# Attention by pairs of heads: two heads' scores in the row halves of the array, their values in its column halves

## What is computed

```python
for window, dilation in DILATED_PATTERNS:          # ((128, 1), (512, 4), (2048, 16))
    o, lse = dilated_window_attention(q, k, v, window, dilation)
...
wts = jax.nn.softmax(jnp.stack(lses), axis=0)
return jnp.einsum('gbsh,gbshd->bshd', wts, jnp.stack(outs))
```

```python
logits = jnp.einsum('bqhgd,bqkhd->bqhgk', qb, ksel).astype(jnp.float32) * att_scale
logits = jnp.where(valid[:, :, None, None, :], logits, -jnp.inf)
prob = jax.nn.softmax(logits, axis=-1)
return jnp.einsum('bqhgk,bqkhd->bqhgd', prob.astype(vsel.dtype), vsel)
```

## Time and profile before

| | us |
|---|---|
| Median of 3 runs | 2689.79 |
| Lowest and highest | 2689.01, 2691.61 |
| The profiled execution, its own time | 2689.53 |
| Its span, first to last instruction | 2687.7 |
| TensorE busy in it | 2562.5 (95%) |
| VectorE, ACT, GpSimd busy | 1155.4, 879.4, 947.8 |
| Mean granted clock of TensorE | 0.976 |

### The profile page before, as it was taken

One profiled execution on the slowest core, in us unless ns is written; L12 is line 12 of the kernel. 1 busy time (PEld: TensorE's weight loads), 2 busy tenths in 40 slices (PEclk: granted clock), 3 DMA queues, 4 the chain that ended last, 5 costly groups with the idle time before them and its releaser, 6 DMA issues.

```text
span 2687.7 us, 29655 instructions
## 1 busy us (share of the span) xinstructions
PE 2562.5 (95%) x11731; PEld 2033.4 (76%) x11731; DVE 1155.4 (43%) x1638; ACT 879.4 (33%) x1102; POOL 947.8 (35%) x205
## 2 busy tenths in 40 slices
PE   5999899999999999899999999989799889999998
PEld 4757688888888757688888887878575578888887
DVE  4445655430312445655430413447585445433301
ACT  4244333431323244333431323341324323322213
POOL 2312234444444312234444443431232134444442
PEclk8999999999999999999999999989899899999999
DMA  3212122222223212122222323220122122222231
GB/s 129 79 32 63 63 77 96 89 99 94 94 94 98 79 32 63 63 79 94 92 96 94 94 94 94 80 63 24 56 76 63 36 79 94 94 94 94 94 102 70
DMA packets 174012, 215.16 MB, mean 80 GB/s; under 512 B 7644, under 2 KB 155028, under 8 KB 173908
## 3 DMA queue, kind: packets, MB, share of 16 engines
q1 hardware_dynamic: 171412, 209.86, 24.3%
q10 hardware_dynamic: 2496, 3.83, 0.4%
HBM read 211.19 MB, written 2.10 MB: 79 GB/s over the span
## 4 chain that ended last, share of the span: by engine, by line
issue 62%; PE 22%; POOL 13%; DVE 1%; ACT 0%; POOLq 0%; DVEq 0%; ACTq 0%
POOL w_lo L276 13%; PE ps L706 6%; PE ps L306 3%; PE ps L307 3%; PE ps L308 3%; PE ps L1694 1%; PE ps L1690 1%; PE ps L1692 1%; PE ps L847 1%; PE ps L826 1%; PE ps L836 0%; DVE s_window L2279 0%; PE ps L2252 0%; POOLq L278 0%; DVE s_pooled L2292 0%
## 5 line engine op out<-in xcount | busy, mean ns | idle before, releaser
L276 POOL TENSOR_TENSOR w_lo<-w_raw,w_hi 128x2048 fp32r<-128x2048 f32 x201 | 947.6, 4715 | 1712.9 <-ACT w_hi L267 1712.9
L267 ACT ACTIVATE w_hi<-w_raw 128x2048 fp32r<-128x2048 f32 x201 | 384.8, 1915 | 1087.9 <-PE ps L308 393.3
L706 PE MATMUL ps<-h_hi,w_hi 128*128 128x512 f32 (+1 forms) x936 | 403.3, 431 | 9.2 <-POOL w_lo L276 5.8
L706 PE MATMUL ps<-h_hi,w_lo 128*128 128x512 f32 (+1 forms) x936 | 374.9, 401 | 0.0
L706 PE MATMUL ps<-h_lo,w_hi 128*128 128x512 f32 (+1 forms) x936 | 374.9, 400 | 0.0
L306 PE MATMUL ps<-h_hi,w_hi 128*128 128x512 f32 x816 | 319.0, 391 | 0.0
L308 PE MATMUL ps<-h_hi,w_lo 128*128 128x512 f32 x816 | 317.5, 389 | 0.0
L307 PE MATMUL ps<-h_lo,w_hi 128*128 128x512 f32 x816 | 317.4, 389 | 0.0
L706 PEld LDWEIGHTS ps<-h_hi,w_hi 128*128 128x128 f32 (+1 forms) x936 | 179.9, 192 | 66.9 <-issue 24.4
L706 PEld LDWEIGHTS ps<-h_lo,w_hi 128*128 128x128 f32 (+1 forms) x936 | 179.9, 192 | 44.5 <-issue 8.6
L706 PEld LDWEIGHTS ps<-h_hi,w_lo 128*128 128x128 f32 (+1 forms) x936 | 179.3, 192 | 43.0
(11 more groups left out here) (399 smaller groups left out, 3935.9 us busy)
## 6 DMA issues: line engine op xcount, KB each, us to landing
w_raw<-in_w_in SPq DMA_DIRECT2D x72, 1024.0 KB, 5.2
w_raw<-in_w_ff SPq DMA_DIRECT2D x64, 1024.0 KB, 5.2
w_raw<-in_w_ffn_in SPq DMA_DIRECT2D x22, 1024.0 KB, 5.0
w_raw<-in_w_out SPq DMA_DIRECT2D x12, 1024.0 KB, 5.1
w_raw<-in_w_ffn_out SPq DMA_DIRECT2D x11, 1024.0 KB, 4.9
w_raw<-in_w_proj_att SPq DMA_DIRECT2D x4, 1024.0 KB, 5.0
w_raw<-in_w_proj_mlstm SPq DMA_DIRECT2D x4, 1024.0 KB, 5.1
w_raw<-in_w_up_ssd SPq DMA_DIRECT2D x4, 1024.0 KB, 5.3
```

Of the source, the lines that this page charges most:

```text
L267: act.activation(k.whi[:, slot * SLOT:(slot + 1) * SLOT], k.wraw[:, slot * SLOT:(slot + 1) * SLOT], ACT.Copy).then_inc(k.hi_done, 1)
L276: pool.tensor_tensor(k.wlo[:, a:a + SLOT], k.wraw[:, a:a + SLOT], k.whi[:, a:a + SLOT], ALU.subtract).then_inc(k.split, 1)
L706: mm = pe.matmul(out, lhs, rhs, start=i == 0 and n == 0, stop=stop and n == 2)
```

## The change

A step is now a pair of heads and a block of queries: 16 steps and 2 or 3 more to drain. The two score matmuls of a pair (L823) follow each other with one semaphore increment on the second, into banks 4 and 5. The value matmuls of both heads (L834) alternate over the blocks of keys, both into bank 7, one head to partitions 0 to 63 and the other to 64 to 127. The transposes (L847) of both heads of step n - 1 stand in step n, each waiting for its multiply and for the copy before. The scores of step n wait for both masks of step n - 1. VectorE has both masks of step n (L867), one reciprocal for both heads of step n - 1 (L874) and its two multiplies (L880). ACT has both exps of step n (L900), the high part of an ended pair (L907) and both copies of step n - 1 (L917). The low part (L885) and the high part are made once a pair over 128 partitions. The side pieces are shared out over three places in each step: behind the scores, behind the place of the values, and between the transposes of the two heads. The budgets are the same.

```diff
     def pe(self, pe):
...
-        for n in range(self.N + 4):
+        for n in range(self.N + 2):
             if n < self.N:
-                h, i = divmod(n, TT)
-                if n >= 2:
-                    pe.wait_ge(*self.at("masked", n - 1))
-                pe.matmul(k.ps[:, 4 + n % 2, 0:(i + 1) * P], self.q(h)[:, i * P:(i + 1) * P],
-                          self.kk(h)[:, 0:(i + 1) * P], start=True, stop=True)\
-                  .then_inc(self.sem("scores"), 1)
-            m = n - 3
+                p, i = divmod(n, TT)
+                if n:
+                    pe.wait_ge(*self.at("masked", 2 * n))
+                for j in range(2):
+                    mm = pe.matmul(k.ps[:, 4 + j, 0:(i + 1) * P], self.q(2 * p + j)[:, i * P:(i + 1) * P],
+                                   self.kk(2 * p + j)[:, 0:(i + 1) * P], start=True, stop=True)
+                mm.then_inc(self.sem("scores"), 1)
+            self.side_pe(pe, 3 * n, self.steps)
+            p = self.ended(n - 2)
+            if p is not None:
+                pe.wait_ge(*self.at("copied", 2 * (n - 1)))
+                if p:
+                    pe.wait_ge(*self.at("lo", p))
+                for b in range(TT):
+                    for j in range(2):
+                        mm = pe.matmul(k.ps[j * HD:(j + 1) * HD, 7, b * P:T], self.v(b, 2 * p + j),
+                                       self.pt[:, (j * TT + b) * T + b * P:(j * TT + b + 1) * T],
+                                       start=b == 0, stop=b == TT - 1, skip_group_check=True)
+                mm.then_inc(self.sem("values"), 1)
+            self.side_pe(pe, 3 * n + 1, self.steps)
+            m = n - 1
             if 0 <= m < self.N:
...
+                for j in range(2):
+                    pe.wait_ge(*self.at("probs", 2 * m + j + 1))
+                    if 2 * m + j:
+                        pe.wait_ge(*self.at("copied", 2 * m + j))
+                    buf = (2 * m + j) % 4 * T
+                    for b in range(m % TT + 1):
+                        tr = pe.transpose(k.ps[:, 6, b * P:(b + 1) * P],
+                                          self.p[:, buf + b * P:buf + (b + 1) * P], k.const(C_ID))
+                    tr.then_inc(self.sem("turned"), 1)
+                    if j == 0:
+                        self.side_pe(pe, 3 * n + 2, self.steps)
...
     def dve(self, dve):
...
                 dve.wait_ge(*self.at("scores", n + 1))
...
+                for j in range(2):
+                    if n:
+                        dve.wait_ge(*self.at("exp", 2 * (n - 1) + j + 1))
+                    c = 2 * n + j
+                    dve.tensor_tensor_reduce(self.ns[:, j * T:j * T + w], k.ps[:, 4 + j, 0:w],
+                                             self.mask(n % TT), 1.0, BIG, ALU.add, ALU.min,
+                                             self.stat[:, c:c + 1]).then_inc(self.sem("masked"), 1)
```

More of the change, by code:

```diff
@@ L796, in __init__ @@
         super().__init__(k, name, prev)
[L797 removed]
+        self.q, self.kk, self.v, self.mask, self.yhi, self.ylo, self.bias = q, kk, v, mask, yhi, ylo, bias
         self.ns = k.at(f"{name}_negscores", ns, 2 * T)
@@ L800, in __init__, with ended, tile @@
         self.pt = k.at(f"{name}_probsT", scr + 4 * T, 2 * TT * T)
-        self.N, self.bias = HEADS * TT, bias
+        self.pairs = HEADS // 2
+        self.N = self.pairs * TT
         self.stat = k.stat
-        self.ends = [self.at("lo", HEADS)]
+        self.ends = [self.at("lo", self.pairs)]
+        self.steps = 3 * (self.N + 2)
     def tally(self):
[L808 to L816, removed]
+        return {**{name: 2 * self.N for name in ("masked", "exp", "probs", "turned", "copied")},
+                "scores": self.N, "recip": self.N, "values": self.pairs, "hi": self.pairs, "lo": self.pairs}
+    def ended(self, n):
+        return n // TT if n >= 0 and n % TT == TT - 1 else None
+    def tile(self, x, p):
+        return x[:, p * T:(p + 1) * T]
     def pe(self, pe):
@@ L889, in act @@
         self.join(act)
[L890 to L891 removed]
+        for n in range(self.N + 2):
+            self.side_out("act", act, 3 * n, self.steps)
             if n < self.N:
                 w = (n % TT + 1) * P
[L894 to L917 removed]
@@ new lines, in act @@
+                for j in range(2):
+                    c = 2 * n + j
+                    act.wait_ge(*self.at("masked", c + 1))
+                    if n >= 2:
+                        act.wait_ge(*self.at("turned", c - 3))
+                    act.activation(self.p[:, c % 4 * T:c % 4 * T + w], self.ns[:, j * T:j * T + w],
+                                   ACT.Exp, bias=self.stat[:, c:c + 1], scale=-1.0,
+                                   accum_out=self.stat[:, 32 + c:33 + c]).then_inc(self.sem("exp"), 1)
@@ new lines, in act @@
+            p = self.ended(n - 2)
+            if p is not None:
+                act.wait_ge(*self.at("values", p + 1))
+                more = {"bias": self.bias(p)} if self.bias else {}
+                act.activation(self.tile(self.yhi, p), k.ps[:, 7, :], ACT.Identity if self.bias else ACT.Copy,
+                               **more).then_inc(self.sem("hi"), 1)
+            m = n - 1
+            if 0 <= m < self.N:
+                p, i = divmod(m, TT)
+                for j in range(2):
+                    act.wait_ge(*self.at("turned", 2 * m + j + 1))
+                    if p and i == 0:
+                        act.wait_ge(*self.at("values", p))
+                    dst = self.pt[:, j * TT * T:(j + 1) * TT * T].rearrange("p (b q) -> p b q", b=TT)
+                    act.activation(dst[:, 0:i + 1, i * P:(i + 1) * P],
+                                   k.ps[:, 6, 0:(i + 1) * P].rearrange("p (b q) -> p b q", q=P),
+                                   ACT.Copy).then_inc(self.sem("copied"), 1)
```

86 lines of the change are left out of this document (18 added, 68 removed).

## The result

The changed kernel takes 2665.32 us (median of 4 runs, 2658.33 to 2668.49) against 2690.70 of the kernel before (4 runs, 2689.01 to 2691.71): a ratio of 0.9903, 95% interval 0.9882 to 0.9923, faster by 1.0%. In six more runs it stood at 0.9928 (0.9915 to 0.9940). The forecast was 2689, no change; its range began at 2666, 0.7 us above the result. The profiled execution took 2666.07 us, its span is 2664.2 (before 2687.7, so 23.5 less).

A forecast was written before the change was run, and what follows sets the result against it. TensorE's matmul queue was taken to set the pace in attention. From 2689.53 us: -18.2 - 36 + 23.3 + 27.8 - 5.6 + 8 = -0.7, so 2689; own range 2676 to 2702, 8-in-10 range 2666 to 2726.

The forecast's parts named there:

- (1): TensorE in attention: fewer groups of half-array matmuls, so fewer switches; 6.1 us saved a stretch, 18.2 in three.
- (2): TensorE in attention: two heads' matmuls overlap in different array halves; scores 3.8, values 8.1 us a stretch, 36 in three.
- (3): Attention: transposes come sooner after their scores, so TensorE waits for masks, multiplies and copies; 23.3 us lost.
- (4): Attention: VectorE's multiplies fall inside GpSimd's w_lo and are held, so transposes start late; 27.8 us lost.
- (5): TensorE's existing idle time in the three attentions, already counted in (3) and (4), goes; 5.6 us saved.
- (6): TensorE's clock drops after three of seven long waits; 8 us lost, bounds 0 and 24.
- far bound: The upper bound of (2), taken as its value: 36 us in three attentions; the other bound was nothing.
- the multiply slips past GpSimd: Rival: in attention multiplies start before w_lo, so most of (4) and all of (6) vanish; 2659 to 2670 us, chance 0.20.
- The halves take turns: Rival: in attention matmuls of different array halves never overlap, so the 36 us are lost; 2725 us, chance 0.27.
- point of decision: For "The halves take turns": decided once fewer than about 10 of the 36 us appear, waits then exceeding savings by over 0.2%.
- Only row halves: Rival: row halves (scores) overlap but column halves (values) don't, so 24 of 36 us are lost; 2713 us, chance 0.10.

The follow-up runs named there:

- both undone: Changed kernel with the values of both heads in one column half and their scores in one row half: 2724.48 us, ratio 1.0128.
- short w_lo: GpSimd's subtract cut from 2,048 to 64 columns for all units but the first two: changed kernel 2568.69 us, kernel before 2610.46 us.
- multiply-first kernel: Changed kernel with VectorE's reciprocal and two multiplies of step n-1 ahead of the masks of step n: 2636.99 us, repeated at 2634.91 us.

## Why the prediction was wrong

By its own steps, for the three attentions, forecast against measured:

| step | forecast | measured | from |
|---|---|---|---|
| (1) fewer switches | -18.2 | -11 to -14 | 62 less the next two; both undone |
| (2) scores side by side | -11.5 | -25.6 | 12 x 2.13, timeline; run 28.5 |
| (2) values side by side | -24.3 | -25.7 | 12 x (4.45 - 2.31); run 25.9 |
| (3) shorter lead | +23.3 | +18.9 | idle time with a short w_lo |
| (4) GpSimd in the way | +27.8 | +22.6 | 41.5 - 18.9 |
| (5) waits of before | -5.6 | -5.4 | 314.50 - 309.06 |
| (6) clock | +8 | +10 | half of 41.0 - 19.9 us at 0.50; what is left of -15.8 |
| outside the attentions | 0 | -7.7 | 23.5 - 15.8 |
| sum | -0.7 | -23.5 | |

Half of the busy time at the lower clock is an estimate of what it cost. By it TensorE's work at full clock is 299.1 us before and 285.8 with both parts undone (318.98 - 66.3 / 2); the 13.3 between them are the second value for (1).

**The step that failed is (2), the scores**: "within a half the two matmuls of an fp32 product follow each other, but the first of the second head may run beside the last of the first. Four slots of scores become three". The runs show two slots: the first matmuls of both heads start within some 10 ns of each other, and then the second ones do. The 36 us were given as the far bound, and the true value, 51, lay beyond it. The mistake was to carry the order of the program (both matmuls of head A's product, then both of head B's) over to the order in which the halves take them. With two slots the same sum gives 2675 us, and the forecast's own range moves to 2662 to 2688, which holds 2665. The other 10 us are the sum of the misses in the rest of the table, above all the 7.7 outside the attentions, a term that was put at nothing without a reason. At 128 columns, where the prediction saw nothing to win because the weight load is as long as the slot, the four matmuls now take two slots as well; in the kernel with the short w_lo:

```profile
168.19 0.49 PE L825 MATMUL ps<-qk 64*128 64x128 f32 x4
168.62 0.50 PE L708 MATMUL ps<-h_hi,w_hi 128*128 128x512 f32 x1
```

0.43 us, and 0.22 of it without the switch.

**What was right.** That column halves overlap and not only row halves: 2.31 us for sixteen, "about 2.3" in the forecast. The rule of the Trainium skill that speaks against it (page "TensorE: Matmul & The Clock Gate", section "Part 3: Packing small matmuls": a weight load overlaps a running matmul only where the row group differs) would, by the prediction's sum, have given 2713 and is not what these runs show: all sixteen use all rows, differ in the column half alone, and take the time of eight. The prediction read that sentence alone; the same section also lets loads into the background weight buffer run ahead, and has 2.38 times the speed for three matmuls in different columns, so it doesn't make this rival true. Its other figure, matmuls in different parts of the array starting some 4 ns apart, is near the 6 or 7 ns between the two records of a pair here.

**A reason that doesn't hold.** The prediction took the far bound "because different halves share neither rows nor columns". By the rows the scores are 64*128 and the values 128*64: two row halves share all columns, two column halves share all rows. They overlap all the same.

**The waits** came where they were forecast and by the forecast mechanism: three multiplies held in each long attention (L880 of 4.49 us and more, where 2 to 4.5 were expected, ending 0.2 us after w_lo), gaps of 4.43, 3.11 and 2.71 us. These gaps hold 10.3 us with their share of (3) in it. What w_lo adds, the idle time less that with a short w_lo, is 9.4 us in a long attention, where 11.3 was forecast, and 3.7 in the third, where it was 5.2. Both terms were 4 to 5 us too high, and which of the steps walked gave too much was not followed further. The multiply-first kernel shows how much hangs on VectorE's order: nothing else changed, and 33 us went, though w_lo still held multiplies.

**The clock** cost 10 us more than before, where 8 was forecast and 0 to 24 allowed. Seven gaps of 2.7 to 4.4 us were each followed by a stretch at 0.50, not the three that were let in, but five of the seven are 3.4 us long and not 6.8.

**Outside the attentions** nothing was forecast, and 7.6 of the 7.7 us lie behind the third. Before, in the pool stage, on VectorE, GpSimd and TensorE:

```profile
2125.20 4.51 POOL L276 TENSOR_TENSOR w_lo<-w_raw,w_hi 128x2048 fp32r<-128x2048 f32 x1 [21.43 <-ACT w_hi L267]
2125.34 4.40 DVE L2292 TENSOR_TENSOR s_pooled<-s_window,s_u 128x16 f32<-128x16 f32 x1
2129.80 2.07 PE L2252 MATMUL ps<-s_pooled,s_pool_w 128*128 128x512 f32 x2 [3.97 <-DVE s_pooled L2292]
```

After:

```profile
2108.93 0.18 DVE L2295 TENSOR_TENSOR s_pooled<-s_window,s_u 128x16 f32<-128x16 f32 x1
2109.87 4.58 POOL L276 TENSOR_TENSOR w_lo<-w_raw,w_hi 128x2048 fp32r<-128x2048 f32 x1 [25.21 <-ACT w_hi L267]
2110.30 1.06 PE L2255 MATMUL ps<-s_pooled,s_pool_w 128*128 128x512 f32 x2
```

An operation on 16 columns, 0.18 us when free, took 4.40 because w_lo had started 0.14 us before it, and TensorE waited 3.97 us. In the changed kernel the same operation comes 0.94 us ahead of w_lo, and the wait and its stretch at the lower clock are gone: by estimate 3.97 us and half of the 5.5 that TensorE was busy in that stretch, 6.7 of the 7.6. With a short w_lo the two kernels need the same time behind the third attention (552.9 and 553.4 us), so the whole difference hangs on w_lo. It is like the third rival of the prediction, "the multiply slips past GpSimd", at a place where nobody had looked for it; that it came out in favour of the change is luck.

**The rivals.** "The halves take turns" was priced at 2725; the kernel in which they do take turns needs 2724.48. That they agree is luck. Of the 35 us above the kernel before, the sum had all in the attentions: 45.5 of idle time, 8 for the clock, -18.2 for the switches. The run has 45 there, 35.3 of idle time, about 23 for the clock and -13 for the switches, and 10 less outside. The rival's point of decision, "fewer than about 10 of the 36 us", is wrong by the prediction's own sum: from -0.7 the time passes +5.4 as soon as 6 of the 36 are missing, so fewer than about 30 decide. It changes nothing here, since 51 appeared. "Only row halves" is false. "The multiply slips past" is false inside the attentions, but for the first of the two multiplies at the last of the three steps.

**What stays open.** The switches between forms saved 11 to 14 us and not 18, though a single switch costs what was read before (0.20 us in and out around the scores at 171.80). The new order cuts the transposes of a step in two with a piece between, and those edges were not counted; no run takes them apart.

## What to carry to other kernels

Two half-array matmuls in different halves cost the time of one here, also where each is an fp32 product of two, if they are neighbours in the queue; put them in turns, and bound such a gain by the whole of the second one. When a change shortens the lead with which results reach TensorE, look at the order on the engine that makes them, however little it is busy: here VectorE's order alone was worth 33 us, more than the change itself. And where GpSimd makes long sweeps, a short VectorE operation on SBUF that others wait for should start right before them, since 0.2 us decided over 4 here.

## What was not expected of the hardware

- The score records of the two heads come in the order first, first, second, second: two products of 512 columns take 1.06 us with the switch out, in one half 1.91.
- In the order head by head the column halves overlap only at the seam: 3.86 us for sixteen value matmuls, 2.31 in turns, 4.45 in one half. There the second head's first record starts ahead of the first head's last three.
- A VectorE operation that starts 0.14 us after GpSimd's subtract of 2,048 columns lasts 4.40 us at only 16 columns with two tensor inputs from SBUF, and one that starts 0.23 us after it lasts 4.49 at 384 columns with one; they end 0.03 and 0.2 us after the subtract. The first started ahead of it in the changed kernel and took 0.18. The masks, which read PSUM, aren't held: the eight of 256 columns that ran inside a w_lo in the changed kernel took 0.42 us, as the others did.
- In the attentions gaps of 2.7 to 4.4 us were each followed by 3.4 or 6.8 us at a granted clock of 0.50; TensorE's busy time was 13.8 us longer than in the kernel with 19.7 us less of idleness.
